# A two-layer trunk on one core: the filling of the delta rule in steps of three matmuls, the gate part inside its own group, and the first value projection in banks 0 and 1

## The chip, the core and the metric

The kernel runs on one core of a Trainium2 chip. The metric is the device time of one execution in microseconds (us). Before the change the median of 3 runs is 1593.56 us (1591.74 to 1597.66). Engines are named as in the profile: PE is TensorE, DVE is VectorE, ACT is ScalarE, POOL is GpSimd and SP is SyncE, whose queue issues most DMAs.

## What is computed

256 tokens of width 1024 pass through two layers and a final RMSNorm, all in float32.

```
layer 0:  x = x + sliding-window attention(rmsnorm(x));  x = x + dense SwiGLU(rmsnorm(x))
layer 1:  x = x + gated DeltaNet(rmsnorm(x));            x = x + top-2-of-8 expert SwiGLU(rmsnorm(x))
```

The change lies in layer 1. Of the DeltaNet, these lines of the reference matter:

```
proj = h @ w_in                                   # 1024 -> q, k (1024 each), v (2048), z (2048), beta, a
qkv = silu(causal_depthwise_conv(qkv, conv_w))    # width 4
a_low = strict lower part of (k_beta @ k.T) * decay, in chunks of 64 tokens, per head
t_inv = inverse of (eye + a_low)
u = t_inv @ (v * beta);  w = t_inv @ (k_beta * exp(gc))
v_new = u - w @ state;  o = q_dec @ state + attn @ v_new;  state = state * decay + k_tail.T @ v_new
o = rmsnorm(o) * norm_g * silu(z);  x = x + o @ w_o
```

## The kernel before

**Dense matmuls.** A weight matrix comes in panels of 128x2048 numbers (1 MB). ACT rounds a panel into `whi` (L627), DVE makes the rest `wlo` (L930), each with three slots, so a panel can be split only when the panel three before it has been used by PE. A product is the sum of three 128x512 matmuls (`triple`, L1421 to L1423). I call such a triple a step. Four steps, one token block against one panel, are a block, and two blocks (b = 0, 1) use up a panel. `AHEAD` says how many panels ACT and DVE split at each place of a group.

**The DeltaNet.** 16 value heads are worked on in four groups of four heads (g = 0 to 3). A group needs 12 blocks of projection, `project(g, i)`: i = 0 to 3 are q and k, 4 to 7 the values v, 8 to 11 the gate z. All are accumulated in PSUM banks 6 and 7 (b = 0, 1). They are copied out with the factor of the RMSNorm: q and k into `group_part(g)` and v into `prj_v` by ACT (L757), z over q and k in `group_part(g)` by DVE (L1088, `z_scaled`), whose SiLU ACT takes in place (L783). A group's output is four blocks of `w_o`, also in banks 6 and 7, which DVE adds to X (L1101).

**The chain of a group.** PE, DVE, ACT and POOL work on one chain: transposes of the projections (L1720), four taps of the convolution (ACT L781, DVE L1110), SiLU, transposes back (L1734, L1746), sums for the decay (L1741), norms, `kk` (L1761), the transposed `qdec` that POOL makes (L1766), the matrix A and its first inverse (DVE, L1773). Then come six levels (lv = 1 to 6), each of which doubles the size of the inverted blocks. A level, for two halves q of the heads:

```
P:   4 matmuls q=0 (L1789)   T: 4 transposes q=0 (L1797)   P: q=1   T: q=1
     DVE copies P into Pc (L1190), ACT copies T into Tc (L826)
     ... filling(6 + lv) ...
dTT: 8 matmuls, both halves (L1807); DVE subtracts them from TT (L1201, four instructions)
     ACT copies even columns of the new TT into Ec (L822), which the next T reads
```

After the levels come the new values, wT, the state and the outputs o, again with copies by ACT (vnew, L833) and DVE in between.

**The filling.** PE does not stand still at these places, because `filling(place)` issues blocks there that do not belong to the chain: the next group's projection and the group before's output. `FILLED[g][place]` is the number of blocks issued by that place, so the finest unit is a block. Groups 0 to 3 hold 12, 16, 16 and 4 blocks. The first group's 12 blocks of projection stand ahead of all this, with 15 products of zeros (`keep_clock`, L1495) between block 3 and block 4, which waits until ACT has emptied banks 6 and 7. Two more such runs (5 and 14 products) stand at the start of group 3.

**The experts.** 8 experts follow, three weight matrices each of 1024x3584. Their panels stream through 14 ring slots straight from HBM; PE uses them as float32 with 32-column tiles (L1884, L1901). SP issues the first ones when the last group's outputs are done (L426, L430). Once per expert, `row_numbers` (L1910) multiplies a 128x144 table, of which one expert's 6 columns are needed. At the end the last expert's rows are added to X by 24 small matmuls (L1988) and DVE (L1403), then squares, rsqrt on POOL (L505), the scaling of both token blocks on DVE (L1412) and two stores.

## Time and profile before

| | |
|---|---|
| median of 3 runs | 1593.56 us (1591.74 to 1597.66) |
| the profiled execution's own time | 1595.22 us |
| its span, first to last instruction | 1593.4 us |
| mean granted clock of TensorE | 0.988 of full speed |
| busy PE / DVE / ACT / POOL | 1529.0 (96%) / 561.5 (35%) / 381.2 (24%) / 185.2 us (12%) |
| chain that ended last | PE 86%, DVE 7%, ACT 3%, POOL 1% |
| moved from and to HBM | 440.87 MB read, 7.34 MB written, 283 GB/s on average |

Three things help in reading it. First, a float32 matmul appears as two instructions (x8 is four matmuls), a triple of fp32r matmuls as three. Second, the duration of a matmul runs until its end leaves the array, while the next one starts long before: what a matmul costs is the distance between two starts. So a stretch can be called busy and still hold time in which PE issues nothing. Third, the profile puts the DeltaNet between 317.7 and 667 us and the experts between 703 and 1578 us; the groups 0 to 3 begin at 346.0, 423.7, 513.2 and 602.4 us.

### The profile page before, as it was taken

How to read it: one execution, taken by the hardware profiler on the slowest of the kernel's cores; microseconds unless marked ns; L12 is line 12 of the kernel's file. 1: busy time of each engine (PE TensorE's matmuls, PEld its weight loads, DVE VectorE, ACT ScalarE, POOL GpSimd, SP SyncE). 2: the span in 40 equal slices, each digit the busy share in tenths (PEclk: the TensorE clock that was granted, in tenths of full speed). 3: DMA queues.
4: the chain of work that ended last, by engine and by line, in shares of the span. 5: the costliest groups of instructions: out<-in, count | busy, mean ns of one | idle time of the engine just before them, and what ended most of it. 6: DMA issues, size and time to landing. Idle time of an engine off the chain costs nothing.

```text
span 1593.4 us, 34961 instructions
## 1 busy us (share of the span) xinstructions
PE 1529.0 (96%) x15647; PEld 912.5 (57%) x15647; DVE 561.5 (35%) x807; ACT 381.2 (24%) x605; POOL 185.2 (12%) x182
## 2 busy tenths in 40 slices
PE   8799999998999998899999999999999999999997
PEld 6677888776877776763443533534444435335344
DVE  4655454557675848342121211212021212111113
ACT  5544444454554535310000000000000000000000
POOL 0100000106152524200000000000000000000100
PEclk9899999999999999999999999999999999999999
DMA  9227555543233200199999999999999999999993
GB/s 349 88 66 258 188 192 184 193 141 114 71 106 101 86 1 1 45 412 415 405 412 407 411 409 408 410 410 408 409 412 398 413 409 405 412 386 412 414 407 137
DMA packets 145354, 450.38 MB, mean 283 GB/s; under 512 B 10624, under 2 KB 41888, under 8 KB 130880
## 3 DMA queue, kind: packets, MB, share of 16 engines
q1 hardware_dynamic: 141680, 437.10, 71.1%
q0 software_dynamic: 3536, 11.14, 1.8%
q8 instruction: 123, 2.02, 0.5%
q14 instruction: 15, 0.12, 0.0%
HBM read 440.87 MB, written 7.34 MB: 281 GB/s over the span
## 4 chain that ended last, share of the span: by engine, by line
PE 86%; DVE 7%; ACT 3%; POOL 1%; SPq 1%; issue 1%; DMA 1%; DVEq 0%; POOLq 0%; ACTq 0%
PE banks L1884 36%; PE banks L1901 18%; PE banks L1421 8%; PE banks L1423 7%; PE banks L1422 7%; PE banks L1797 2%; PE banks L1807 1%; DVE cvall L1110 1%; DVE wlo L930 1%; ACT whi L627 1%; DMA par<-in_attn_sinks_dram 1%; DVE TT L1201 1%; PE banks L1789 1%; PE banks L1841 1%; POOL qdec L539 1%
## 5 line engine op out<-in xcount | busy, mean ns | idle before, releaser
L1884 PE MATMUL banks<-ring,xg 128*32 128x512 f32 (+1 forms) x6144 | 583.2, 539 | 0.0
L1884 PEld LDWEIGHTS banks<-ring,xg 128*32 128x32 f32 x6144 | 199.1, 110 | 367.9 <-issue 331.3
L1246 DVE TENSOR_TENSOR ehid<-banks,esil 64x768 f32<-64x768 f32 (+1 forms) x64 | 89.5, 1398 | 715.1 <-ACT esil L859 714.6
L1901 PE MATMUL banks<-ring,ehT 128*32 128x256 f32 x5376 | 296.1, 379 | 0.0
L1901 PEld LDWEIGHTS banks<-ring,ehT 128*32 128x32 f32 x5376 | 173.6, 110 | 122.3 <-issue 9.7
L859 ACT ACTIVATE esil<-banks 64x1536 f32<-64x1536 f32 (+1 forms) x32 | 41.0, 1282 | 777.9 <-PE banks L1884 777.9
L930 DVE TENSOR_TENSOR wlo<-raw,whi 128x2048 fp32r<-128x2048 f32 x74 | 178.6, 2415 | 77.4 <-ACT whi L627 77.0
L1421 PE MATMUL banks<-whi,xhi 128*128 128x512 f32 x448 | 180.9, 404 | 8.5 <-issue 2.3
L1423 PE MATMUL banks<-whi,xlo 128*128 128x512 f32 x448 | 175.9, 393 | 0.0
L1422 PE MATMUL banks<-wlo,xhi 128*128 128x512 f32 x448 | 175.7, 392 | 0.0
L627 ACT CAST whi<-raw 128x2048 fp32r<-128x2048 f32 x74 | 141.2, 1908 | 49.0 <-PE banks L1423 43.6
L1421 PEld LDWEIGHTS banks<-whi,xhi 128*128 128x128 f32 x448 | 84.6, 189 | 30.0 <-issue 4.9
L1423 PEld LDWEIGHTS banks<-whi,xlo 128*128 128x128 f32 x448 | 84.7, 189 | 18.3
L1422 PEld LDWEIGHTS banks<-wlo,xhi 128*128 128x128 f32 x448 | 84.8, 189 | 16.1
L502 POOL TENSOR_SCALAR par<-par 128x4 f32<-128x4 f32 (+2 forms) x17 | 3.3, 195 | 475.9 <-ACT squares L641 245.7
L585 POOL TENSOR_TENSOR rowcol<-par 128x1 f32<-128x1 f32 x8 | 1.6, 198 | 372.6 <-ACT yrow L876 372.6
L593 POOL TENSOR_TENSOR rowcol<-par 128x1 f32<-128x1 f32 x7 | 1.3, 191 | 365.6 <-DVE next_rows L1304 365.6
L1201 DVE TENSOR_TENSOR TT<-TT,banks 128x128 f32<-128x128 f32 x96 | 22.3, 284 | 59.6 <-PE banks L1807 59.1
L1110 DVE SCALAR_TENSOR_TENSOR cvall<-banks,par,cvall 128x255 f32<-128x255 f32 (+2 forms) x96 | 39.5, 474 | 0.6
L1421 PE MATMUL banks<-whi,hhi 128*128 128x512 f32 x88 | 34.9, 397 | 1.4 <-DVE hlo L1044 1.4
L1422 PE MATMUL banks<-wlo,hhi 128*128 128x512 f32 x88 | 34.7, 395 | 0.0
L1423 PE MATMUL banks<-whi,hlo 128*128 128x512 f32 x88 | 34.7, 394 | 0.0
(304 smaller groups left out, 1296.5 us busy)
## 6 DMA issues: line engine op xcount, KB each, us to landing
ring<-in_moe_w_gate_dram SPq DMA_DIRECT2D x112, 1024.0 KB, 14.8
ring<-in_moe_w_up_dram SPq DMA_DIRECT2D x112, 1024.0 KB, 15.5
ring<-in_moe_w_down_dram SPq DMA_DIRECT2D x112, 1024.0 KB, 14.2
raw<-in_dn_w_in_dram SPq DMA_DIRECT2D x16, 1024.0 KB, 5.1
raw<-in_ffn_w_gate_dram SPq DMA_DIRECT2D x22, 512.0 KB, 4.0
raw<-in_ffn_w_up_dram SPq DMA_DIRECT2D x22, 512.0 KB, 5.0
raw<-in_ffn_w_down_dram SPq DMA_DIRECT2D x11, 1024.0 KB, 4.9
raw<-in_dn_w_in_dram SPq DMA_DIRECT2D x16, 512.0 KB, 4.9
```

Source lines behind the costliest of these rows:

```text
L627: act.copy(slot(whi, n, SPLIT), slot(raw, n, RAW)).then_inc(hi_ready, 1)
L859: act.activation(esil[64:P, :, 0:n_], src[0:64, :, 0:n_], ACT.Silu).then_inc(sem("esil_ready"), 1)
L930: dve.tensor_tensor(slot(wlo, n, SPLIT), slot(raw, n, RAW), slot(whi, n, SPLIT).bitcast(F32), ALU.subtract).then_inc(lo_ready, 1)
L1110: i = dve.scalar_tensor_tensor(out=cvall[:, t, s_:], in0=conv_src(t)[:, 0:SEQ - s_], scalar=tap(g, t, w), in1=cvall[:, t, s_:], op0=ALU.mu ...
L1201: dve.tensor_tensor(t_, t_, d_, ALU.subtract).then_inc(sem("TT_ready"), 1)
L1246: i = dve.tensor_tensor(ehid[64 * s:64 * s + 64, 0:TILES * n_ // 2].rearrange("p (t k j) -> p t k j", t=TILES, k=k_), by_row(src, s), by_r ...
L1421: pe.matmul(ps, lhs_hi, wh, start=start, stop=False)
L1422: pe.matmul(ps, lhs_hi, wl, start=False, stop=False)
L1423: return pe.matmul(ps, lhs_lo, wh, start=False, stop=stop)
L1797: i = pe.matmul(bank[q][64 * b:64 * b + 64, h % 2 * P:(h % 2 + 1) * P], (Ec if lv < LEVELS - 1 else TT)[:, 4 * b + h, 0:64], ident, start= ...
L1884: last = pe.matmul(bank[first_bank + t][TILE * q:TILE * (q + 1), 0:n_].rearrange("p (s c) -> p s c", s=2), xg[:, t, kt, :], w[q // 2][:, k ...
L1901: i = pe.matmul(token_tile(3, t, q, 256), eT[:, h_:h_ + TILE], w[:, at_:at_ + 256], start=first and m == 0 and k == 0 and t % 2 == 0, stop ...
```

## The change

1. **Filling in steps.** `FILLED` now counts steps (triples). Inside a level there are two places, one between T and dTT as before and a new one after dTT. There are two late places, after wT and before the second block's new values. The matmuls of a level stand in the order P, P, T, T instead of P, T, P, T.
2. **Gate part in its own group.** Blocks 8 to 11 of `project(g, i)` are the first four blocks of group g's filling, rather than part of what stands ahead of it. Groups 0 to 3 now hold 48, 64, 64 and 32 steps (12, 16, 16 and 8 blocks); ahead of group 0 stand 8 blocks instead of 12. The order of the panels follows.
3. **Copies.** z goes through one ACT instruction per block straight from PSUM, scale and SiLU together (`gate_silu`), after the second convolution SiLU; DVE's `z_scaled` is gone. DVE copies v (`projected_v`), once per group, before its work on the second block's outputs. ACT copies q and k one block at a time, in levels 2 and 3. DVE adds the second half of an output one block at a time.
4. **First group.** Its v blocks go to banks 0 and 1, so block 4 waits for no copy. The 15 products of zeros are gone, and so are the 5 and 14 in group 3.
5. **ahead(9)**, the late split of a panel on ACT and DVE, stands behind the copy of the second block's new values instead of ahead of it.
6. **Experts.** `row_numbers` multiplies only the 6 columns that are needed.
7. **End.** DVE makes a part of `ylast`. The 24 matmuls go through the four row tiles in turn instead of tile by tile; DVE adds 512 columns at a time (4 instead of 8). ACT scales block 0 of the result, DVE block 1, and DVE multiplies block 0 by the gain while POOL makes the rsqrt.

The diff's core:

```diff
-        FILLED = ((2, 3, 4, 5, 6, 7, 7, 8, 9, 10, 11, 12, 12, 12), (2, 3, 4, 5, 6, 8, 9, 10, 11, 12, 13, 14, 15, 16),
-                  (2, 3, 4, 5, 6, 8, 9, 10, 11, 12, 13, 14, 15, 16), (0, 0, 1, 2, 3, 4, 4, 4, 4, 4, 4, 4, 4, 4))
-        AHEAD = ((4, 5, 6, 6, 7, 7, 8, 8, 9, 9), (4, 5, 6, 7, 8, 8, 9, 9, 10, 11), (4, 5, 6, 7, 8, 8, 9, 9, 10, 11),
-                 (3, 3, 4, 4, 4, 4, 4, 4, 4, 4))
+        STEPS = 4
+        FULL_GROUP = ((8, 12, 16, 20, 24, 29, 32), ((34, 36), (38, 40), (42, 44), (46, 48), (50, 53), (56, 58)), (61, 64))
+        FILLED = (((8, 12, 16, 20, 22, 25, 26), ((27, 28), (30, 32), (33, 35), (36, 38), (39, 41), (43, 44)), (46, 48)),
+                  FULL_GROUP, FULL_GROUP,
+                  ((6, 10, 16, 20, 24, 25, 26), ((27, 27), (28, 28), (29, 29), (30, 30), (31, 31), (32, 32)), (32, 32)))
+        QK_BLOCK0, OUT_BLOCK0 = (1, 2, 3, 5), (4, 6, 7)
+        QK_PART_AT, OUTPUTS_AT = (2, 3), ((0, 0), (4, 5), (4, 5), (3, 6))
+        AHEAD = ((4, 5, 6, 6, 6, 7, 7, 7, 8, 9), (4, 5, 6, 7, 7, 8, 8, 9, 10, 11), (4, 5, 6, 7, 7, 8, 8, 9, 10, 11),
+                 (4, 5, 6, 6, 6, 6, 6, 6, 6, 6))
...
-            def projected(g, part):
-                act.wait_ge(panel_used, PROJ[g, 2 * part + 1] + 1)
...
+            def projected_qk(g, b):
+                act.wait_ge(*((panel_used, PROJ[g, 1] + 1) if b else (sem("block0_psum"), QK_BLOCK0[g])))
+                act.activation(group_part(g)[:, b, :], bank[6 + b], ACT.Copy, scale=rs[:, b:b + 1])\
+                    .then_inc(sem("prj_qk_ready"), 1)
+
+            def first_projected_v():
+                act.wait_ge(panel_used, PROJ[0, 3] + 1)
+                for b in range(TB):
+                    i = act.activation(prj_v[:, b, :], bank[b], ACT.Copy, scale=rs[:, b:b + 1])
+                i.then_inc(sem("prj_v_ready"), 1)
+
+            def gate_silu(g):
+                act.wait_ge(panel_used, PROJ[g, 5] + 1)
+                for b in range(TB):
+                    i = act.activation(group_part(g)[:, b, :], bank[6 + b], ACT.Silu, scale=rs[:, b:b + 1])
+                i.then_inc(sem("z_ready"), 1)
...
-                    if more and lv == 1:
-                        projected(g + 1, 1)
+                    for b in range(TB):
+                        if more and lv == QK_PART_AT[b]:
+                            projected_qk(g + 1, b)
...
+            dve.wait_ge(panel_used, final * EP + (P_MOE + EP))
+            dve.tensor_copy(ylast[:, 512:768], bank[4][:, 0:256]).then_inc(sem("ylast_ready"), 1)
...
+                    i_ = triple(bank[b if first_v else 6 + b], *xT(kt, b), nn, slice(k * 512, (k + 1) * 512), kt == 0, kt == KT - 1)
+                if STEPS - 1 in steps:
+                    if b == 1:
+                        i_.then_inc(panel_used, 1)
+                    elif m == 1:
+                        i_.then_inc(sem("block0_psum"), 1)
...
-            for i in range(12):
-                if i == 4:
-                    keep_clock(15, bank[0])
...
+                def fill_to(count):
+                    while done[0] < count:
+                        k, first = divmod(done[0], STEPS)
+                        end = min(STEPS, first + count - done[0])
+                        steps = range(first, end)
+                        if k < 4:
+                            project(g, 8 + k, steps)
+                        elif g == 0:
+                            project(1, k - 4, steps)
+                        elif g == GROUPS - 1:
+                            output_between(g - 1, k - 4, steps)
+                        elif k in (4, 5, 10, 11):
+                            output_between(g - 1, k - 4 if k < 6 else k - 8, steps)
+                        else:
+                            project(g + 1, k - 6 if k < 10 else k - 8, steps)
+                        done[0] += end - first
...
-                if g == GROUPS - 1:
-                    pe.wait_ge(sem("z_scaled"), GROUPS)
-                    keep_clock(5, bank[6])
                 if g:
                     outputs_T(g - 1)
                 filling(1)
-                if g == GROUPS - 1:
-                    keep_clock(14, bank[6])
...
+                    for q in range(2):
...
-                    filling(6 + lv)
+                    filling_level(lv, 0)
...
+                    filling_level(lv, 1)
...
-                filling(13)
+                filling_late(0)
...
+                        filling_late(1)
...
-                    i = pe.matmul(numbers[:, 0:TURNS * 2 * TILES], sel32[:, b, :], tilerow[:, b, :, :].rearrange("p e t -> p (e t)"),
...
-                for q in range(4):
-                    p_ = slice(TILE * q, TILE * (q + 1))
-                    for t in range(TILES):
...
+                for t in range(TILES):
+                    for q in range(4):
+                        p_ = slice(TILE * q, TILE * (q + 1))
```

In a level of group 1, on PE. Names: `Ac` and `Ec` are even columns of A and TT; L1807 is dTT, L1789 P and L1797 T. Before:

```order
L1422 MATMUL banks<-wlo,xhi 128x512
L1423 MATMUL banks<-whi,xlo 128x512
L1807 MATMUL banks<-Pc,Tc 128x64 x8
L1789 MATMUL banks<-TT,Ac_110 64x64 x4
L1797 MATMUL banks<-tabs,Ec 64x128 x4
L1789 MATMUL banks<-TT,Ac_110 64x64 x4
L1797 MATMUL banks<-tabs,Ec 64x128 x4
L1421 MATMUL banks<-whi,xhi 128x512
```

With the change (L1849 is dTT, L1830 P, L1839 T, L1452 to L1454 a step):

```order
L1849 MATMUL banks<-Pc,Tc 128x64 x8
L1452 MATMUL banks<-whi,xhi 128x512
L1453 MATMUL banks<-wlo,xhi 128x512
L1454 MATMUL banks<-whi,xlo 128x512
L1452 MATMUL banks<-whi,xhi 128x512
L1453 MATMUL banks<-wlo,xhi 128x512
L1454 MATMUL banks<-whi,xlo 128x512
L1830 MATMUL banks<-TT,Ac_110 64x64 x8
L1839 MATMUL banks<-tabs,Ec 64x128 x8
L1452 MATMUL banks<-whi,xhi 128x512
```

Two steps moved from between T and dTT to between dTT and the next P; the other two stayed.

The start of group 3 on PE, before:

```order
L1720 MATMUL banks<-tabs,oall_92 128x128 x8
L1720 MATMUL banks<-tabs,prj_v 128x128 x8
L1495 MATMUL banks<-spare 128x512 x5
L1685 MATMUL banks<-tabs,oall_91 128x128 x8
L1495 MATMUL banks<-spare 128x512 x14
L1734 MATMUL banks<-tabs,cvall 128x128 x8
```

With the change:

```order
L1766 MATMUL banks<-tabs,oall_92 128x128 x8
L1766 MATMUL banks<-tabs,prj_v 128x128 x8
L1452 MATMUL banks<-whi,xhi 128x512
L1453 MATMUL banks<-wlo,xhi 128x512
L1454 MATMUL banks<-whi,xlo 128x512
```

Where the zeros stood there are six steps of the gate part, and four more behind the transposes of the outputs.

ACT in group 1, levels 1 to 3 (L822 and L842 are Ec, L826 and L846 Tc, L627 and L635 the split of a panel). Before:

```order
L822 COPY Ec<-TT 128x128 x4
L826 COPY Tc<-banks 128x256 x2
L757 ACTIVATE prj_v<-banks,par 128x512 x2
L627 CAST whi<-raw 128x2048
L822 COPY Ec<-TT 128x128 x4
L826 COPY Tc<-banks 128x256 x2
```

With the change:

```order
L842 COPY Ec<-TT 128x128 x4
L846 COPY Tc<-banks 128x256 x2
L635 CAST whi<-raw 128x2048
L842 COPY Ec<-TT 128x128 x4
L846 COPY Tc<-banks 128x256 x2
L764 ACTIVATE oall_91<-banks,par 128x512
L842 COPY Ec<-TT 128x128 x4
L846 COPY Tc<-banks 128x256 x2
L764 ACTIVATE oall_91<-banks,par 128x512
```

No more than one of the two kinds of work now stands between a level's copies and the next level's.

## Rows read from the trace of the kernel before

**Rows 1.** Windows: stretch, its length, busy us (instructions) per engine; clock, DMA share, GB/s

```profile
317.70:346.00 28.30, 26.56 (x117) 21.21 (x117) 12.70 (x11) 14.21 (x15) 2.04 (x2) 1.00 0.44 152
346.00:381.10 35.10, 29.84 (x153) 23.70 (x151) 32.90 (x46) 22.37 (x29) 16.72 (x12) 1.00 0.42 137
381.10:414.40 33.30, 31.60 (x349) 25.18 (x349) 15.81 (x39) 15.17 (x37) 9.54 (x8) 1.00 0.30 96
423.70:461.00 37.30, 36.00 (x187) 28.97 (x185) 34.77 (x51) 23.41 (x41) 19.31 (x15) 1.00 0.18 57
461.00:500.20 39.20, 35.82 (x361) 28.37 (x360) 17.52 (x43) 16.57 (x34) 8.47 (x7) 0.96 0.33 108
513.20:602.40 89.20, 82.99 (x630) 67.77 (x628) 59.26 (x98) 45.08 (x88) 32.35 (x24) 0.98 0.15 48
602.40:635.70 33.30, 27.46 (x145) 21.25 (x143) 27.51 (x50) 18.04 (x34) 13.91 (x14) 1.00 0.00 1
635.70:657.20 21.50, 18.57 (x289) 15.84 (x289) 12.79 (x39) 8.99 (x32) 8.04 (x7) 0.92 0.01 2
703.30:1578.00 874.70, 874.70 (x11559) 377.66 (x11558) 140.21 (x164) 49.19 (x51) 48.18 (x62) 1.00 1.01 402
```

**Rows 2.** Waits of PE from 346 to 667 us: total us, times, longest

```profile
PE banks L1841 <- ACT vnew L833: 4.4, 4, 1.5
PE banks L1797 <- ACT Ec L822: 3.7, 2, 1.8
```

**Rows 3.** Timeline, level 4 of group 1: start, length, engine, line

```profile
482.11 0.45 PE L1789 MATMUL banks<-TT,Ac 128*64 128x64 f32 x8
482.64 0.66 PE L1797 MATMUL banks<-tabs,Ec 128*64 128x128 f32 x8
483.13 0.40 PE L1789 MATMUL banks<-TT,Ac 128*64 128x64 f32 x8
483.36 0.61 PE L1797 MATMUL banks<-tabs,Ec 128*64 128x128 f32 x8
483.90 0.50 PE L1421 MATMUL banks<-whi,xhi 128*128 128x512 f32 x1
484.23 0.39 PE L1422 MATMUL banks<-wlo,xhi 128*128 128x512 f32 x1
...
486.86 1.11 PE L1807 MATMUL banks<-Pc,Tc 64*128 64x64 f32 x16
487.57 0.93 DVE L1201 TENSOR_TENSOR TT<-TT,banks 128x128 f32<-128x128 f32 x4 [3.47 <-PE banks L1807]
488.11 0.45 PE L1789 MATMUL banks<-TT,Ac 128*64 128x64 f32 x8
```

**Rows 4.** Timeline, the zeros in the first group's projection, and DVE's first taps

```profile
317.74 3.56 PE L1495 MATMUL banks<-spare 128*128 128x512 f32 x15
...
348.42 5.01 DVE L1110 SCALAR_TENSOR_TENSOR cvall<-banks,par,cvall 128x255 f32<-128x255 f32 x12
```

**Rows 5.** Groups of the page, the split of a panel on DVE and on ACT

```profile
L930 DVE TENSOR_TENSOR wlo<-raw,whi 128x2048 fp32r<-128x2048 f32 x74 | 178.6, 2415 | 77.4 <-ACT whi L627 77.0
...
L627 ACT CAST whi<-raw 128x2048 fp32r<-128x2048 f32 x74 | 141.2, 1908 | 49.0 <-PE banks L1423 43.6
```

**Rows 6.** Chain that ended last, around the first row_numbers: start, length

```profile
703.30 10.44 PE banks L1884 x96
714.43 31.04 PE banks L1884 x288
```

**Rows 7.** Timeline, the end: last expert's rows added, both blocks scaled

```profile
1579.32 5.35 PE L1988 MATMUL banks<-ylast,selTr 32*128 32x256 f32 x48 [0.98 <-ACT ylast L876]
...
1587.85 2.48 DVE L1412 SCALAR_TENSOR_TENSOR H<-X,par,gain 128x1024 f32<-128x1024 f32 x2 [1.20 <-POOL par L505]
```

**Rows 8.** Windows of 2 us, before the clock falls in group 1 and after

```profile
466.00:468.00 2.00, 1.00 (x18) 0.72 (x16) 0.88 (x4) 2.00 (x3) 0.00 (x0) 1.00 0.44 171
...
470.00:472.00 2.00, 2.00 (x17) 1.57 (x15) 1.32 (x3) 1.09 (x3) 0.99 (x1) 0.50 0.06 12
```

More of the change, by code:

```diff
@@ L296, in out_panel @@
             panels.append((dn_w_o[g * 512:g * 512 + 512, h * 512:h * 512 + 512].rearrange("(k p) n -> p k n", p=P),))
-        for m in range(6):
+        for m in range(4):
             project_panel(0, m)
@@ L302, in trunk @@
             LIST.append(len(panels))
-            for m in range(6):
+            for m in (4, 5):
+                project_panel(g, m)
+            for half in range(2):
+                if g:
+                    out_panel(g - 1, half)
                 if g + 1 < GROUPS:
-                    project_panel(g + 1, m)
-                if g and m in (1, 3):
-                    out_panel(g - 1, m // 2)
+                    project_panel(g + 1, 2 * half)
+                    project_panel(g + 1, 2 * half + 1)
         for h in range(2):
@@ L1687, in outputs_T @@
                     i.then_inc(sem("on_psum"), 1)
-            for i in range(12):
-                if i == 4:
-                    keep_clock(15, bank[0])
+            for i in range(8):
                 project(0, i)
```

169 lines of the change are left out of this document (84 added, 85 removed).

## The prediction

> **What bounds the kernel now.** I looked first at the chain that ended last: 86% of it is PE. So I took windows by stage [rows 1]. From 703.3 to 1578 us, in the experts, PE is busy for all of 874.7 us: nothing upstream is hidden there, and what the DeltaNet gives back shows in full at the end, since SP starts the experts' weights when the last group's outputs are done. In the DeltaNet's windows PE is busy for 82 to 97%, which looks like little to gain. The waits [rows 2] name only a few us: 4.4 us in front of L1841 (ACT's copy of vnew) and 3.7 us in front of L1797 (Ec). The timeline of one level [rows 3] shows why this understates it. From 482.11 to 488.11 a level takes 6.00 us. Its filling, 12 matmuls, runs from 483.90 to 486.86. Then dTT's 16 instructions start at 486.86, DVE begins to subtract 0.71 us later, and P can start only at 488.11, 1.25 us after dTT. P's 8 instructions are issued in 0.23 us (483.13 to 483.36), so dTT's 16 take some 0.46 us. The other 0.8 us PE issues nothing, though it counts as busy. A second hole is between P and T of q = 0: 0.53 us where the issue takes 0.23. This pattern stands in all 24 levels. That is what the finer filling is aimed at; PE's own work is the floor.
>
> **Prices.** A 128x512 matmul costs 0.23 us: 15 zeros in 3.56 us, of which the last one's end is 0.4 [rows 4]. A step is then 0.69 us and a block 2.76 us. The block in the level took 2.96 us, and its first matmul 0.33 instead of 0.23 [rows 3]: going into and out of a filling costs about 0.2 us. A bare level's own issue is P 2 x 0.23, T 2 x 0.49 (483.36 to 483.90, less some of the switch) and dTT 0.46, together 1.90 us; with two fillings of 0.2 and 0.05 for the rest, 2.35 us plus 0.69 per step.
>
> **A rule that speaks against two fillings per level.** T, the steps, dTT and P use the array in different tilings (128x64, 128x128, 64x128, 128x64), and the change makes four changes of tiling per level out of three. By [rows 3] the pair of changes costs 0.2 us. The Trainium skill (TensorEngine Tiling, Key Properties) says that a change of the tiling mode drains TensorE. If each change cost the whole tail of a matmul (0.39 of duration less 0.23 of distance), a filling would cost 0.32 us, 24 levels 2.9 us more, and the sum would end at 1557.8 instead of 1554.9 us. The row is a measurement of just these changes, so I keep 0.2.
>
> **The sum, stage by stage.**
>
> *First group's projection, 317.7 to 346.0.* 28.3 us for 8 blocks and the zeros [rows 1]. Four blocks stay (11.0 us, no wait for a copy) and the sums for the gates (0.3): 11.3, so **-17.0 us**. Of this 11.0 is only moved: the four gate blocks are in group 0's filling now, and each later group's likewise, which leaves one group's four blocks extra in group 3. Real gains here are the 15 zeros (3.5) and the waits.
>
> *Group 0, 346.0 to 423.7.* Its start is bound by the chain on DVE, not by PE: DVE is busy for 32.9 of 35.1 us [rows 1]. From the first tap at 348.42 [rows 4] to the first level at 381.1 are 32.7 us. One split of a panel stood between the two halves of the taps (2.3 us and 0.8 idle before it); it is ahead of them now, so 29.8. But the taps begin later after the group's start than the 2.4 us of before. The last v matmul is at 328.7, then ACT copies (1.3), splits a panel (1.9), DVE splits it (2.3) [rows 5] and has 0.3 of small work: taps at 334.5, levels at 364.3, with 0.7 for POOL's qdec 365.0. That is 36.0 us from the start of the group at 329.0 instead of 35.1: +1.0 rounded. The levels: 6 x 2.35 + 18 x 0.69 + 0.5 (levels too short for a DVE split) = 27.0 against 33.3: -6.3. After them four steps more: 2.8 + 0.2 = +3.0. Together **-2.3**.
>
> *Groups 1 and 2.* The start of group 1 (37.3 us) holds 36 steps now and 32 with the change: -2.8 if PE sets it. But what was behind kk (A, T, T0 on DVE and PE) has a chain of its own, so I take -2.3; the ends are 0 and -2.8. Levels: 6 x 2.35 + 26 x 0.69 = 32.0 against 39.2: **-7.2**. Of that some 1.6 is the clock (0.96 in this window [rows 1]): it fell to half after two us in which PE was busy 1.00 of 2.00 us, waiting for an Ec that stood on ACT behind a copy of v and a split [rows 2, 8]. With the change no such pair stands there. After the levels: vnew's copy of the second block no longer waits behind ahead(9) (longest wait 1.5, -0.9), two steps more (+1.4) and the second late filling's entry (+0.1): +0.6. Group 1 **-8.9**. Group 2 has the same length as group 1 (89.2 us [rows 1]), the same tables and waits: **-8.9**.
>
> *Group 3.* 16 steps more and 19 zeros fewer. Its start (33.3 us, PE busy 27.5, including zeros of 4.4) has 26 steps where 16 were: +6.9 - 4.4 of PE work in 5.8 us of idle time, and the same chain on DVE (27.5 of 33.3 busy), which still begins behind the second block's outputs. -0.4; the ends are -1.5 and +2.5. The levels held no filling after the second; now one step each, and with so little the wait behind dTT stays: 0.69 + 0.2 - 0.1 (the new order of P and T) = 0.8 per level, +4.8; of the clock (0.92, so 1.7 us) and the first level's wait I take 1.2 back: +3.6 on 21.5. **+3.2**. The adds of the earlier outputs that DVE moved to levels 3 and 6 are 0.6 us each beside this.
>
> *Experts.* Between two expert products row_numbers takes 714.43 - 713.74 = 0.69 us [rows 6]. With 6 columns each of its four instructions still costs about the 0.11 us of a small one (48 in 5.35 us in [rows 7]), 0.44 together; 8 times 0.25 is **-2.0**. Ends: 0 and -5.5. The weights' stream would have to keep up; the DMA share is 1.01 in that window, PE waits for no weights, and 0.25 us in 109 is nothing.
>
> *End.* DVE takes ylast's smaller part, -0.35. PE's 24 matmuls take 5.35 us in order of tiles [rows 7]; with four row tiles in turn between 2.7 (twice as dense, the density of the experts' column tiles) and 5.35. Then four adds of 512 columns, 0.62 each by the 2.48 us for twice 1024: the last ends some 4.2 us after PE's start, before 5.9. -1.7. The first block's scaling goes to ACT, so the last store is issued 1.2 us earlier, but both stores share the DMA: -0.7. **-2.8**; ends 0 and -3.8.
>
> Sum: -17.0 - 2.3 - 8.9 - 8.9 + 3.2 - 2.0 - 2.8 = **-38.7 us**. Against the profiled execution's own 1595.22 us that is 1556.5 (its span of 1593.4 becomes 1554.7). The median of the runs, 1593.56, is 1.7 below that execution, so I predict **1554.9 us**.
>
> **Rivals.**
>
> *The in-order queues pay part of it back (0.20).* ACT and DVE take a panel's split of 1.9 and 2.3 us in one piece, and a level is to shrink from 6.0 to about 5.1. In a level with both a split and an add on DVE, Pc comes at about 0.7 + 0.9 + 2.3 + 0.6 + 0.5 = 5.0 us after dTT. If Pc or Ec is late by 0.6 us in the 18 levels of groups 0 to 2 (+10) and group 0's start is 5 us longer because POOL's qdec finds less filling in front of it (22 steps instead of 24), the time is 1570. For it: DVE is busy for 33 of 35 us in group 0's start. Against: within the levels it is busy for 17.5 of 39.2 us.
>
> *Everything uncovered (0.05).* If the chain also shortens by what it waited for PE, group 3's levels cost nothing for their steps (-4.8), the starts of groups 1 and 2 give all (-1.0) and group 0's start is 3 us shorter: 1546.
>
> *DVE's chain sets the groups (0.08).* Then the filling moves but the groups do not shorten, and only the zeros ahead of group 0 (3.6), the experts' 2.0 and the end's 2.8 are gained: 1585, at the edge of no change. Against it: in group 1 PE's idle time before its levels is 1.3 of 37.3 us, and levels take 6.00 us with a filling block that alone is 2.96.
>
> *The clock (0.03), slower.* 34 products of zeros that kept PE active go, at the entrance of the layer and in group 3. Where PE was sparsely used the granted clock fell to half, 1.2 GHz: after the 1.00 of 2.00 us of [rows 8]. If group 0's start and group 3 ran at that level, every step there would cost 0.69 us more. With 26 + 32 steps that is 40 us, and another 18 for the chain's own matmuls: 1613. It decides once the doubling costs more than the 38.7 gained plus 8. Against: real steps take the zeros' place, and in group 3's start, idle for 5.8 us, the clock stayed at 1.00. The Trainium skill (TensorE: Matmul & The Clock Gate, What's actually happening) says that the throttled state is the default and activity releases it; by that rule the zeros' removal alone would be the danger, and the filling in their place the cure.
>
> My forecast takes the remaining 0.64.
>
> **Numbers.** The range goes from 1546 to 1573: below, the uncovered case; above, the in-order rival with the bounds of group 3 and the end added. Faster by over 0.5% (8 us, about what a measurement of this kernel can tell from no change): the forecast, the first two rivals and a part of the third, 0.92; within 0.5%: 0.05; slower: 0.03.
>
> **What would show it.** Right: levels of groups 1 and 2 of about 5.1 us each, with P starting straight behind the second filling; group 0 starting at about 329 and first level at about 365; no clock below 1.00 in group 1's levels; groups of about 80 us; the experts unchanged but for 0.4 us between L1884 and L1901 with the numbers. Wrong: levels over 5.5 us with waits for Pc or Ec, group 0's first level later than 370, or a clock under 0.9 over a whole group. If the levels are right and the time isn't, look at PE's wait for POOL's qdec and for A.

## The result, and the profile after

The changed kernel takes 1573.04 us (median of 4 runs, 1571.4 to 1576.36), the kernel before 1595.20 on the same chip (4 runs, 1591.74 to 1597.66). The ratio is 0.9861, 95% interval 0.984 to 0.9882: 22 us, 1.4% faster. The sign was forecast, the size not: -22 us instead of -38.7, and 1573.04 lies just beyond the range's upper end of 1573.

The windows by stage of the changed kernel (stretch, length, busy us and instructions of PE, PEld, DVE, ACT, POOL, then clock, DMA share, GB/s) answer to [rows 1]:

```profile
317.70:329.05 11.35, 11.35 (x54) 9.38 (x52) 6.93 (x7) 9.07 (x11) 2.04 (x2) 1.00 0.57 201
329.05:365.08 36.03, 28.95 (x148) 22.27 (x146) 32.91 (x47) 22.59 (x31) 16.78 (x12) 1.00 0.40 130
365.08:395.80 30.72, 30.09 (x343) 23.10 (x343) 13.77 (x39) 13.61 (x36) 8.64 (x8) 1.00 0.21 70
395.80:407.55 11.75, 11.07 (x85) 10.37 (x85) 6.04 (x7) 5.19 (x13) 4.65 (x4) 1.00 0.28 91
407.55:443.19 35.64, 34.02 (x175) 26.56 (x173) 34.12 (x50) 21.67 (x38) 18.59 (x14) 1.00 0.27 89
443.19:478.73 35.54, 35.54 (x367) 27.64 (x367) 19.27 (x43) 17.36 (x38) 9.69 (x9) 1.00 0.39 119
478.73:491.85 13.12, 12.45 (x92) 11.50 (x91) 5.36 (x7) 5.19 (x13) 3.95 (x3) 1.00 0.26 81
...
576.09:612.47 36.38, 30.77 (x156) 23.85 (x155) 34.04 (x50) 21.63 (x38) 18.51 (x14) 0.95 0.00 1
612.47:637.37 24.90, 23.55 (x306) 18.42 (x306) 12.17 (x39) 8.92 (x32) 8.01 (x7) 0.93 0.01 2
637.37:646.60 9.23, 8.55 (x73) 8.22 (x73) 2.62 (x4) 3.39 (x12) 1.20 (x2) 1.00 0.00 0
```

Each group has three rows: its start, its levels, what follows them. In group 1's levels PE is busy for 35.54 of 35.54 us and the profile names no wait of PE there, and still they take 35.5 us, not the 32.0 of the forecast. In group 3's start PE is busy for 30.77 of 36.38, with a clock below 1.00. Against before:

| stretch | forecast | measured | of it |
|---|---|---|---|
| first group's projection | -17.0 | -16.9 | 28.3 to 11.35 |
| group 0 | -2.3 | +0.8 | start 36.0 as forecast, levels 30.7 for 27.0 |
| group 1 | -8.9 | -5.2 | start 35.6 for 35.0, levels 35.5 for 32.0 |
| group 2 | -8.9 | -5.0 | as group 1 |
| group 3 | +3.2 | +6.5 | start 36.4 for 32.9, levels 24.9 for 25.1 |
| from its outputs to the experts | 0 | 0.0 | |
| experts | -2.0 | -1.2 | 0.54 us per row_numbers, 0.44 forecast |
| end | -2.8 | -1.0 | |
| sum | -38.7 | -22.0 | spans 1593.4 and 1571.4 |

One level of group 1 with four steps, the changed kernel's timeline (start, length, engine, line, operation), for [rows 3]. The weight loads (PEld) are shown with it:

```profile
454.62 0.55 PEld L1830 LDWEIGHTS banks<-TT,Ac 128*64 128x64 f32 x16 [0.36 <-issue]
454.62 0.69 PE L1830 MATMUL banks<-TT,Ac 128*64 128x64 f32 x16
...
455.14 1.05 PE L1839 MATMUL banks<-tabs,Ec 128*64 128x128 f32 x16
...
456.12 0.50 PE L1452 MATMUL banks<-whi,onhi 128*128 128x512 f32 x1
...
457.70 0.97 PEld L1849 LDWEIGHTS banks<-Pc,Tc 64*128 64x128 f32 x16 [0.37 <-issue]
457.71 1.11 PE L1849 MATMUL banks<-Pc,Tc 64*128 64x64 f32 x16
458.42 0.93 DVE L1229 TENSOR_TENSOR TT<-TT,banks 128x128 f32<-128x128 f32 x4 [2.77 <-PE banks L1849]
...
458.75 0.50 PE L1452 MATMUL banks<-whi,onhi 128*128 128x512 f32 x1
...
460.34 0.45 PE L1830 MATMUL banks<-TT,Ac 128*64 128x64 f32 x8
```

From P to P it is 0.52 for P, 0.98 for T, 1.59 for a filling of two steps, 1.04 for dTT (457.71 to 458.75) and 1.59 again: 5.72 us. P and dTT both have 16 matmuls with 64 moving columns; P's weight loads of 64 columns take 0.55 us together, dTT's of 128 columns 0.97. The kernel before had the same row, which I hadn't read:

```profile
486.86 0.97 PEld L1807 LDWEIGHTS banks<-Pc,Tc 64*128 64x128 f32 x16 [0.35 <-issue]
488.10 0.31 PEld L1789 LDWEIGHTS banks<-TT,Ac 128*64 128x64 f32 x8 [0.28 <-DVE TT L1201]
```

So of the 1.25 us between dTT and P [rows 3] 1.04 were dTT itself, and the hole that a second filling can hide was 0.2 us, as much as going into and out of that filling costs.

### The profile page after: what moved, and what is told of

Read it like the earlier page. It is cut to its first block, busy times and chain, and to the rows that moved or that the text cites. A ratio compares the mean times of both kernels' runs of the same rounds, so it can differ in the third digit from the quotient of the medians.

```text
span 1571.4 us, 34876 instructions
## 1 busy us (share of the span) xinstructions
PE 1516.2 (96%) x15613; PEld 897.7 (57%) x15613; DVE 560.7 (36%) x802; ACT 378.9 (24%) x603; POOL 189.1 (12%) x182
## 4 chain that ended last, share of the span: by engine, by line
PE 86%; DVE 8%; issue 2%; ACT 1%; SPq 1%; DMA 1%; POOL 1%; POOLq 0%; DVEq 0%; ACTq 0%
PE banks L1929 37%; PE banks L1946 19%; PE banks L1452 8%; PE banks L1454 7%; PE banks L1453 7%; PE banks L1849 1%; PE banks L1839 1%; DVE cvall L1139 1%; DVE wlo L955 1%; PE banks L1830 1%; DMA par<-in_attn_sinks_dram 1%; DVE T L1199 1%; SPq L409 1%; PE banks L1886 1%; PE banks L1858 0%
## 5 line engine op out<-in xcount | busy, mean ns | idle before, releaser
L1452 PE MATMUL banks<-whi,xhi 128*128 128x512 f32 x448 | 183.0, 409 | 4.6 <-issue 2.3
L1454 PE MATMUL banks<-whi,xlo 128*128 128x512 f32 x448 | 176.1, 393 | 0.0
L635 ACT CAST whi<-raw 128x2048 fp32r<-128x2048 f32 x74 | 141.1, 1906 | 47.1 <-PE banks L1454 41.8
L1452 PEld LDWEIGHTS banks<-whi,xhi 128*128 128x128 f32 x448 | 84.7, 189 | 24.7 <-issue 5.4
L1454 PEld LDWEIGHTS banks<-whi,xlo 128*128 128x128 f32 x448 | 84.6, 189 | 18.5
L1452 PE MATMUL banks<-whi,hhi 128*128 128x512 f32 x88 | 34.9, 397 | 1.4 <-DVE hlo L1069 1.4
L1454 PE MATMUL banks<-whi,hlo 128*128 128x512 f32 x88 | 34.7, 394 | 0.0
```

Source lines behind the costliest of these rows:

```text
L635: act.copy(slot(whi, n, SPLIT), slot(raw, n, RAW)).then_inc(hi_ready, 1)
L1452: pe.matmul(ps, lhs_hi, wh, start=start, stop=False)
L1454: return pe.matmul(ps, lhs_lo, wh, start=False, stop=stop)
```

## Experiments

14 kernels, on several chips. A kernel is compared with the kernel before on the same chip, by the ratio; the changed kernel's experts take 873.6 us on one chip and 881 to 885 on others, so traces are compared stage by stage ahead of them. Where a table or a sentence says "groups", it is the time from group 0's first transpose to the transposes of group 3's outputs: 324.7 us before, 321.9 in the changed kernel.

### One filling or two, and the order of P and T

`one_filling` removes the last line of a level:

```diff
                         i.then_inc(sem("dTT_psum"), 1)
-                    filling_level(lv, 1)
```

> The changed kernel with the filling behind dTT left out in all 24 levels: its steps go to the next level's filling behind T (the last two of a group to the place after the levels), the order P, P, T, T stays. The same steps in all, 18 fillings fewer. Theory A (PE's own work: dTT's 16 instructions cost 1.04 us and the hole behind them is only 0.2, as much as going into and out of a filling costs): a level with four steps stays at 5.7 us from P to P, the time within 3 us of the changed kernel's 1573. Theory B (my prediction's price: dTT 0.46, hole 0.8): levels of 6.3 us, 18 times 0.6 = 11 us longer, 1584. Theory C (the second filling is what keeps Ec and the clock from getting in the way): waits for Ec behind ACT's splits come back in some levels and the granted clock falls in groups 1 and 2, 3 to 6 us longer, with the undisturbed levels at 5.7.

`alternate_order` removes the second loop over q:

```diff
                         i.then_inc(sem("P_psum"), 1)
-                    for q in range(2):
                         if lv < LEVELS - 1:
                             pe.wait_ge(sem("Ec_ready"), ...)
```

> The changed kernel with P and T in the order of before, P T P T instead of P P T T, with both fillings kept. Theory A (the 0.3 us between P and T of before was the wait for Ec, which the filling behind dTT now covers as well): a level of four steps stays at 5.7 us, 1573, within 1 us. Theory B (the order itself costs, by changing between P and T three times instead of once): 0.3 per level, 24 levels, 7 us longer, 1580.

`one_filling_alternate` has both edits.

> Both undone together, so that a level is built as before (P T P T, one filling), all else as changed. Theory A: a level of four steps takes 6.0 us again, 0.3 more than with either alone, 18 times 0.3 = 5.4 us and, in group 3, which had one filling already, 6 times 0.3 = 1.8; with waits for Ec at half clock up to 3 more: 1580 to 1583. Theory B (the fillings were worth 0.6 a level and the order 0.1): 1586 or more. If the effects of the two simply add up from the runs of each alone, their gains are of different causes; by A they don't add, each alone costs nothing.

Starts of P of a four-step level, and the distance to the next:

| | level, us | ratio to before | groups, us |
|---|---|---|---|
| two fillings, P P T T (the change) | 5.71 | 0.9861 (0.9840 to 0.9882) | 321.9 |
| two fillings, P T P T | 5.71 | 0.9848 (0.9831 to 0.9864) | 321.3 |
| one filling, P P T T | 5.93 | 0.9879 (0.9863 to 0.9896) | 326.4 |
| one filling, P T P T | 6.01 | 0.9904 (0.9887 to 0.9920) | 328.6 |

Two levels of `one_filling` in its timeline:

```profile
455.59 1.11 PE L1849 MATMUL banks<-Pc,Tc 64*128 64x64 f32 x16
456.84 0.90 PE L1830 MATMUL banks<-TT,Ac 128*64 128x64 f32 x16
457.56 1.05 PE L1839 MATMUL banks<-tabs,Ec 128*64 128x128 f32 x16
461.52 1.11 PE L1849 MATMUL banks<-Pc,Tc 64*128 64x64 f32 x16
462.77 0.90 PE L1830 MATMUL banks<-TT,Ac 128*64 128x64 f32 x16
```

P follows dTT after 1.25 us as before the change, and P's 16 now stretch from 0.52 to 0.72 us (456.84 to 457.56): its second half waits for TT of the second half of the heads. So one filling costs 0.2 us per level and 4.5 us over the groups, where A expected nothing and B 0.6 per level. The order alone costs nothing while the second filling is there, and 0.1 when it isn't: the 0.3 us between P and T of [rows 3] were a wait for Ec and TT that either edit mostly covers, and the gains of the two don't add up. A holds with a correction of 0.2; B and, in the levels, C don't: the granted clock stayed at 1.00 in both groups' levels. Notice that the level of 9.35 us of before didn't come back in any of the four.

### dTT doubled

```diff
-                        for h in (2 * q, 2 * q + 1):
+                        for h in (2 * q, 2 * q + 1, 2 * q, 2 * q + 1):
                             for b in range(TB):
                                 k_ = slice(64 * b, 64 * b + 64)
```

> The changed kernel with dTT's 16 matmuls of each level issued twice, the same result written again. Theory A (each pair of them costs 0.11 us, since each loads 128 columns of weights): 24 times 0.9 = 21.6 us longer, 1594.6, and the levels of group 1 at 6.6 us. Theory B (0.46 us as for P's 16): 24 times 0.46 = 11 us, 1584, levels at 6.2.

Measured: 1594.49 us, ratio 0.9977 (0.9968 to 0.9987); four-step levels of 6.60 us, 0.90 more. In PE's timeline dTT has 32 matmuls in 2.00 us:

```profile
457.70 2.00 PE L1849 MATMUL banks<-Pc,Tc 64*128 64x64 f32 x32
461.23 0.69 PE L1830 MATMUL banks<-TT,Ac 128*64 128x64 f32 x16
464.31 2.00 PE L1849 MATMUL banks<-Pc,Tc 64*128 64x64 f32 x32
```

A: 0.90 us per level, the price that I had at 0.46. That the time agrees with A's 1594.6 as well is luck: the kernel before took 1598.09 us on this chip, and the groups grew by 20.4 us (342.3 for 321.9), not by 21.6.

### The level of 9.35 us in the kernel before

```diff
-                 ... (4, 5, 6, 7, 8, 8, 9, 9, 10, 11), (4, 5, 6, 7, 8, 8, 9, 9, 10, 11), ...
+                 ... (4, 5, 6, 6, 7, 8, 9, 9, 10, 11), (4, 5, 6, 6, 7, 8, 9, 9, 10, 11), ...
```

(`AHEAD` of groups 1 and 2, in the kernel before.)

> The kernel before with one panel of groups 1 and 2 split a level later (after level 2 instead of level 1), so that ACT has no copy of v and split in a row in front of level 2's Ec. Theory A (of the 7.2 us that each of these groups' levels had over the changed kernel's, 3.3 are one level's wait for Ec and the half clock behind it): the level of 9.35 and 9.15 us becomes 6.0 to 6.3, no clock below 1.00 in groups 1 and 2, 6 us less than before, ratio 0.996. Theory B (the fall of the clock comes from something else, as the zeros or the bursts of the experts' weights): it stays in level 2 or moves to another, the ratio is 0.999 to 1.001.

The 7.2 us in this expectation is the forecast's figure; the levels of group 1 differed by 3.7 (39.2 and 35.5). Measured: ratio 0.9960 (0.9946 to 0.9974), as A said. The levels of group 1 take 5.76, 6.01, 6.01, 5.98, 5.98 and 6.16 us where they took 5.76, 9.35, 6.01, 6.00, 5.99 and 6.15; in the windows of both groups' levels the clock is 1.00:

```profile
461.00:497.00 36.00, 34.32 (x362) 27.23 (x361) 17.75 (x43) 16.63 (x34) 8.22 (x7) 1.00 0.36 118
547.00:583.00 36.00, 34.32 (x362) 27.21 (x362) 17.75 (x43) 16.63 (x34) 8.22 (x7) 1.00 0.09 30
```

Two copies and a split in a row on ACT thus cost 6.5 us in two groups, by a wait of 1.8 us and the half clock behind it. The changed kernel is rid of this since DVE copies v out and ACT's two copies of q and k stand in different levels; that is 3.3 of the 3.7 us that group 1's levels got shorter. No run undoes this part of the change alone; but the level stays away in the four kernels of the table above, whatever their fillings and order.

### P, P, T, T in the kernel before

```diff
                         i.then_inc(sem("P_psum"), 1)
+                    for q in range(2):
                         if lv < LEVELS - 1:
                             pe.wait_ge(sem("Ec_ready"), ...)
```

> The kernel before with P, P, T, T in each level instead of P, T, P, T and nothing else. Theory A, sized by the runs of one filling in either order (5.9 and 6.0 us): 0.1 per level, 2.4 us, the levels with the wait for Ec stay at 9 us: ratio 0.998 to 1.000. Theory B (the whole 0.3 us between P and T of before goes): 7 us, 0.9955.

Measured: ratio 0.9989 (0.9977 to 1.0001), four-step levels of 5.90 us instead of 6.00. The long level of group 1 took 7.54, that of group 2 10.37. A's size; for the time itself a gain isn't told from none.

### Group 3's start

In the changed kernel DVE's timeline shows a panel's split in front of A:

```profile
602.95 2.92 DVE L955 TENSOR_TENSOR wlo<-raw,whi 128x2048 fp32r<-128x2048 f32 x1
605.80 1.27 DVE L1193 TENSOR_TENSOR A<-banks,EB 128x512 f32<-128x512 f32 x2
607.11 2.59 DVE L1199 TENSOR_TENSOR T<-A,tabs 128x512 f32<-128x512 f32 x2
```

In the kernel before DVE had no split between vb and A and waited for kk there:

```profile
629.89 1.29 DVE L1165 TENSOR_TENSOR A<-banks,EB 128x512 f32<-128x512 f32 x2 [4.95 <-PE banks L1761]
631.21 1.75 DVE L1171 TENSOR_TENSOR T<-A,tabs 128x512 f32<-128x512 f32 x2
```

PE's timeline in the changed kernel:

```profile
608.69 0.77 PE L1814 MATMUL banks<-tabs,T 128*128 128x128 f32 x4 [3.12 <-DVE T L1199]
```

PE waits 3.1 us for T. The panel (group 3's first output panel) is not used before the group's end.

```diff
-                 (4, 5, 6, 6, 6, 6, 6, 6, 6, 6))
+                 (4, 4, 5, 6, 6, 6, 6, 6, 6, 6))
```

> The changed kernel with one panel of group 3 split by DVE behind TT instead of in front of A. Theory A (the fifth panel's split, 2.9 us, stands on DVE in front of A while kk is already there at 603.5): A starts 1.9 to 2.3 us earlier, PE's wait of 3.1 us for T shrinks to about 1, and with it goes the fall of the clock behind it, 1.5 us more: group 3 takes 66.5 to 68.5 us instead of 70.5, 1569 to 1571. Theory B (POOL's masks and qdec set this stretch, DVE only waits beside them): A comes earlier but T0 doesn't, no change within 1 us, 1573.

Measured: ratio 0.9831 (0.9815 to 0.9848). DVE's timeline now has A 1.8 us after the add's start, where the changed kernel has 4.1 (601.75 to 605.80):

```profile
600.42 1.28 DVE L1125 TENSOR_TENSOR X<-X,banks 128x512 f32<-128x512 f32 x2
602.21 1.29 DVE L1193 TENSOR_TENSOR A<-banks,EB 128x512 f32<-128x512 f32 x2 [0.51 <-PE banks L1802]
603.53 2.82 DVE L1199 TENSOR_TENSOR T<-A,tabs 128x512 f32<-128x512 f32 x2
```

PE's waits from 560 to 610 us (us in total, times, longest):

```profile
PE banks L1814 <- DVE T L1199: 1.5, 2, 1.1
PE banks L1830 <- DVE TT L1208: 1.4, 1, 1.4
```

The longest wait for T is 1.1 us, a wait of 1.4 for TT is new, and the clock stays at 1.00. Groups: 319.2 us, 2.7 less. Theory A, at the small end of its range. A now starts 27.5 us after the group does, as in the kernel before (27.5; the changed kernel 29.7). Group 3's start takes 34.4 us instead of 36.4, and the 1.1 us that it still is above before's 33.3 are in T: DVE's two operations take 2.82 us here and 2.59 in the changed kernel, 1.75 before. What slows them no run shows.

### Steps moved to the starts

```diff
-        FILLED = (((8, 12, 16, 20, 22, 25, 26), ((27, 28), (30, 32), (33, 35), (36, 38), (39, 41), (43, 44)), ...
+        FILLED = (((8, 12, 16, 20, 24, 26, 28), ((29, 30), (32, 33), (34, 36), (37, 39), (40, 42), (43, 44)), ...
-                  ((6, 10, 16, 20, 24, 25, 26), ((27, 27), (28, 28), (29, 29), (30, 30), (31, 31), (32, 32)), ...
+                  ((6, 10, 16, 20, 24, 26, 29), ((29, 29), (30, 30), (31, 31), (32, 32), (32, 32), (32, 32)), ...
```

with the split moved as well.

> The changed kernel with group 3's split moved as in the run before, two steps of group 0 put in front of kk and two more before its levels, and in group 3 one and four more before the levels (29 instead of 26 of its 32 steps there), so that levels have fewer. Theory A (PE waits in these starts: 3.5 us for qdec, 1.4 for TT, 3.1 for T; a step there is free, and in a level it costs 0.69): group 0 1.5 to 2.5 us shorter, group 3 1 to 2 shorter than with the split alone; 5 to 7 us less than the changed kernel, ratio 0.981 to 0.983 to before. Theory B (what follows only gets later by what is put in): no more than the split's own 2.7 us, ratio 0.984 to 0.9845.

Measured: ratio 0.9834 (0.9814 to 0.9854), groups 316.5 us, 2.7 less than with the split alone: group 0 77.1 us for 78.5, group 3 1.4 less. In the trace A holds, just below and at the small end of its two ranges. In the time it isn't seen: the interval is 0.2% to either side, and between group 3's outputs and the experts this run took 34.15 us where the changed kernel's took 32.5. That stage has the same code in all sixteen kernels. It took 32.5 to 32.6 us in eleven of them, each with a granted clock of 0.95, and 34.1 to 34.2 in five, each with 0.90. So the longer stage goes with a lower clock; what makes the clock fall further in those five is open.

### dTT in quarters

Each pair's load of 128 columns is cut in two, on 64 x 64 tiles:

```diff
-                            for b in range(TB):
+                            for c, b in ((0, 0), (0, 1), (1, 0), (1, 1)):
                                 k_ = slice(64 * b, 64 * b + 64)
-                                i = pe.matmul(bank[2 + 2 * b + q][:, h % 2 * 64:(h % 2 + 1) * 64], Tc[k_, h, :], Pc[k_, h, :],
-                                              start=True, stop=True)
+                                i = pe.matmul(bank[2 + 2 * b + q][64 * c:64 * c + 64, h % 2 * 64:(h % 2 + 1) * 64],
+                                              Tc[k_, h, 64 * c:64 * c + 64], Pc[k_, h, :], start=True, stop=True)
```

> The changed kernel with each of dTT's matmuls cut in two by columns of its weights: 32 of 64 x 64 instead of 16 of 64 rows x 128 columns, the same products and results. Theory A (the load of 128 columns is what a pair waits for, and four quarters load at the pace at which P's pairs of 64 columns do, 0.058 us): dTT takes 0.5 us instead of 1.0, levels of 5.2 us, 24 times 0.5 = 12 us less, 1561. Theory B (quarters of the same rows load one after the other): 16 pairs at 0.058 = 0.93, no change, 1573. Theory C (another tiling mode costs more at each change): above 1575.

Measured: ratio 0.9798 (0.9781 to 0.9814), four-step levels of 5.31 us, groups 312.9 us, 9.0 less. The weight loads of dTT in its timeline:

```profile
448.15 0.56 PEld L1849 LDWEIGHTS banks<-Pc,Tc 64*64 64x64 f32 x32 [0.36 <-issue]
```

Twice the instructions load in 0.56 us instead of 0.97: four quarters start every 0.058 us, as P's pairs do. A in kind; 0.40 per level instead of 0.5. The quarters are tiled by rows too, as dTT's pairs were, so it isn't tiling by rows that costs: what changed is the columns of each load and how many loads run side by side.

### Where the first term comes from

The prediction called the 15 products of zeros [rows 4] a real cost of 3.5 us. `before_no_zeros` is the kernel before without these 15 and the 19 of group 3's start, products that no result uses:

```diff
-                if i == 4:
-                    keep_clock(15, bank[0])
                 project(0, i)
```

> The kernel before without the 15 products of zeros in front of the first group's seventh to twelfth block and without the 5 and 14 in the start of group 3; nothing else changes. Theory A (the first 15 are plain PE work in front of everything, 3.5 us; the other 19, 4.4 us, stand where PE waits for DVE anyway): 3.5 to 4.5 us less than before, ratio 0.9972 to 0.9978, no new fall of the clock. Theory B (they keep the clock up, as their name says): a half clock of 3 us or more appears in the start of group 0 or of group 3, and half or more of the 3.5 is lost: ratio above 0.9985.

Measured: ratio 1.0036 (1.0022 to 1.0051), slower. PE's longest wait in front of group 0 (us in total, times, longest):

```profile
PE banks L1421 <- ACT oall L757: 3.6, 1, 3.6
```

The windows of that wait and of what follows it, columns as in [rows 1]:

```profile
317.70:319.70 2.00, 0.00 (x0) 0.00 (x0) 0.62 (x2) 2.00 (x2) 1.72 (x2) 1.00 0.35 135
319.70:323.10 3.40, 2.64 (x6) 2.17 (x7) 3.34 (x2) 2.50 (x3) 0.32 (x1) 0.57 0.00 0
```

The zeros filled a wait for ACT's copies out of banks 6 and 7, and without them the clock fell to 0.57: group 0 starts at 346.33 us, not earlier than with them (345.95). Group 3's start takes 35.4 us instead of 33.3; its window from 615 to 633 us has a clock of 0.85. In the kernel before, B was right: without the zeros nothing was gained. How much they earned is less clear. In its trace group 0 starts 0.4 us later and is 0.9 us longer, and group 3 is 0.8 us longer: 2.0 together. A further 1.5 us stands in group 2, 1.6 between the groups and the experts, and 2.5 in the last stage (17.9 us for 15.4), where the code is the same and the clock was lower. The last 24 matmuls took 5.35 us in [rows 7] at a clock of 1.00, and here, at 0.66:

```profile
1594.19 7.82 PE L1983 MATMUL banks<-ylast,selTr 32*128 32x256 f32 x48 [0.98 <-ACT ylast L876]
```

`before_split_later`, which has all its zeros, has the same long last stage (18.1 us), so it also comes where no zeros are missing.

Two kernels then take the changed one apart: `v_in_banks_6_7` (`first_v = False`, and ACT reads banks 6 and 7) and `zeros_back` (`keep_clock(15, bank[2])` in front of the fifth block).

> The changed kernel with the first group's value projection in banks 6 and 7 again, and still no zeros in front of it. Theory A (the other banks are the gain: the fifth block no longer waits for ACT to copy the first four out of banks 6 and 7, behind a panel's split): PE waits 3.4 us or more there, the clock falls to half for a window behind it, group 0 starts 4 to 6 us later than 329.05, and the time is longer by that: ratio 0.989 to 0.990 to before. Theory B (the zeros were the cost, as my prediction put it): group 0 starts within 1.5 us of 329, ratio 0.986 to 0.987.

> The changed kernel with the 15 products of zeros back in front of the fifth block (into bank 2), and the value projection in banks 0 and 1 as changed. Theory A (with the other banks nothing is waited for, so that they are plain PE work): group 0 starts 3.5 us later, 332.5, and the time is 3.5 us longer, ratio 0.9883. Theory B (ACT's and DVE's own work in front of group 0 sets its first level, not PE): the first level comes less than 1.5 us later than 365.1, ratio under 0.987.

Measured: ratios 0.9904 (0.9887 to 0.9921) and 0.9888 (0.9872 to 0.9905). Without the other banks PE waits 3.0 us and the clock is at 0.67 behind it; the first level starts at 369.93 us instead of 365.08. With the zeros back it starts at 367.70; their row

```profile
316.70 3.56 PE L1526 MATMUL banks<-spare 128*128 128x512 f32 x15
```

shows that they are plain work there, though they begin a microsecond earlier than the changed kernel gets to this place. A in kind both times, with smaller sizes: group 0 starts 3.7 us later (332.71) instead of 4 to 6, after a wait of 3.0 instead of 3.4, and with the zeros 2.4 later (331.48) instead of 3.5. In both traces the clock also fell in group 0's start (0.91 and 0.95 over it, 1.00 in the changed kernel). The banks take the wait away, and only then are the zeros a cost.

### The last gain

```diff
-            dve.tensor_tensor(H3[:, 0, :], X[:, 0, :], gain3[:, :], ALU.mult).then_inc(sem("gained"), 1)
+            for q in range(8):
+                i = dve.tensor_tensor(H3[:, 0, q * P:(q + 1) * P], X[:, 0, q * P:(q + 1) * P], gain3[:, q * P:(q + 1) * P], ALU.mult)
+            i.then_inc(sem("gained"), 1)
```

> The changed kernel with the multiplication by the last gain (first block, 1024 columns, 1.22 us on DVE) cut into eight of 128 columns. Theory A (POOL's first small operation of the last 1/rms takes 1.08 us instead of 0.18 because it can't get at the memory while DVE's one long operation runs): it takes 0.2 to 0.4 us now, and the last stage becomes 0.4 to 0.8 us shorter (14.4 us from the last expert's product to the end). Theory B (POOL's operation is long for another reason): it stays at 1.1, and the end comes 0.3 to 0.5 us later, by the seven more instructions.

POOL's timeline has its first operation of the last 1/rms. In the changed kernel:

```profile
1563.96 1.08 POOL L510 TENSOR_SCALAR par<-par 128x2 f32<-128x2 f32 x1 [82.37 <-DVE par L1439]
```

In the kernel before:

```profile
1586.75 0.18 POOL L502 TENSOR_SCALAR par<-par 128x2 f32<-128x2 f32 x1 [84.78 <-DVE par L1408]
```

In this one:

```profile
1573.58 0.35 POOL L510 TENSOR_SCALAR par<-par 128x2 f32<-128x2 f32 x1 [83.22 <-DVE par L1439]
```

The last stage takes 13.94 us instead of 14.40. A. The ratio of 2 runs, 0.9857 (0.9833 to 0.9880), can't show it.

### All of it together

> The changed kernel with all that has been tried for it: dTT in quarters, group 3's split later, the steps moved to the starts, the gain in eighths. If the gains add up (dTT 9.0 us within the four groups, split 2.7, steps 3, end 0.5): 15 us less than the changed kernel, 1558, ratio 0.977. If shorter levels only bring out DVE's and ACT's work behind them (a level of 5.3 us with a split on both): 11 us less, ratio 0.979.

Measured: 1570.51 us where before took 1606.83, ratio 0.9778 (0.9761 to 0.9795), groups 308.2 us and the end 13.94. The groups gave 13.7 of the 14.7 us expected, in spite of a new wait of 1.5 us for Pc in group 3; the stage behind them took 34.2 us, 1.7 more than in the changed kernel's trace. The ratio's interval holds both expectations, 0.977 and 0.979; by the groups the gains nearly add up. It is faster than both kernels: 2.2% than before, some 0.8% than the changed one, whose ratio is 0.9861.

## Why the prediction was right in sign and wrong in size

- **"P's 8 instructions are issued in 0.23 us, so dTT's 16 take some 0.46 us. The other 0.8 us PE issues nothing."** This step failed. dTT's 16 take 1.04 us (and `dtt_twice` added 0.90 per level), since they load 128 columns each and P's load 64. A bare level with two fillings is 0.52 + 0.98 + 1.04 + 0.42 = 2.96 us, not 2.35. Six levels of groups 0, 1 and 2 each are 3.6 us longer by it, 10.8 in all: with it alone the forecast would have been 1565.7 us, inside the range. Of the 16.7 us between forecast and measured spans, these are 10.8, group 3's start is 3.5, the end 1.8 and the experts 0.8; the rest nearly cancels. The columns stand in PEld's row; I had read the matmuls' row only. The Trainium skill (TensorE: Matmul & The Clock Gate, LDWEIGHTS (loading the stationary operand)) has the rule: a weight load's time goes by its columns, not by its rows. The traces agree: 0.112 us from pair to pair with 128 columns, 0.058 with 64.
- **The finer filling in the levels** was therefore worth 0.3 us per level of four steps (6.01 to 5.71), not 0.9, and the second filling and the new order largely cover the same waits. Of the 3.7 us that group 1's levels gained, 3.3 came from the level with the wait for Ec. The six finer levels gave 1.8 more, and two more steps took 1.4 of it back. I had seen that pair on ACT and that the change parts it, but priced it at 1.6.
- **"Going into and out of a filling costs about 0.2 us", against the rule that each change of tiling drains TensorE.** Right: a filling of two steps takes 1.59 us, 0.21 more than 1.38. The 0.32 by the rule would have given 1557.8, nearer to the result for a reason that isn't the one.
- **"The same chain on DVE" in group 3's start, -0.4.** Failed by 3.5 us. The chain is the same, but `AHEAD` now puts two splits of 2.9 us behind vb, where DVE was idle for 4.95 us before; the second stands in front of A, which comes 2.2 us later, and T then takes 0.8 us longer. With one entry of the table changed, the start got 2.0 us shorter and the groups 2.7. The rival of the in-order queues named 1570 us, close to the result, but by another way: Pc or Ec late in 18 levels and a start of group 0 that is 5 us longer. PE waits for no Ec now, for Pc once (0.6 us, in group 0), and that start takes 36.0 us as forecast. Only in group 3's start was the rival's kind of delay there, so its number is near by luck.
- **First group's projection, -17.0, and group 0's start, 36.0 us.** Both right (16.9 and 36.0), but the reason was half of it. The sum took 3.5 us for the zeros as a gain of their own and "no wait for a copy" beside it. Taken alone the zeros gain nothing, since they stand in that wait; they are a cost only once the other banks have removed it. The rival of the clock, which had the zeros keep it up, named what happened in the kernel before without them. In the changed one steps stand in their place, and it was wrong: no clock under 1.00 in group 0, and 0.95 and 0.93 in group 3's start and levels, where the levels of before had 0.92.
- **Small terms.** Starts of groups 1 and 2: 0.6 us too low each; what follows the levels of groups 0 to 2: 0.5 too high each. Experts: 0.54 us per row_numbers instead of 0.44, 0.8 in all. The end: the adds finish 5.4 us after the last expert's product instead of 7.2, as forecast, but POOL's small operation gives 0.9 back, taking 1.08 us instead of 0.18 while DVE multiplies, for which the sum had nothing. (The end's 1.0 us is against a trace in which the last 24 matmuls ran at full clock, 15.4 us in all; in two other kernels with the same last stage it took 17.9 and 18.1, and in the changed kernel and its variants never more than 14.4.) And where the last store followed DVE's last scaling by 3.1 us before (1590.3 to 1593.4), it takes 4.2 now (1567.2 to 1571.4): both stores are issued together, so of the 1.2 us of earlier scaling that I counted on 1.1 are lost, not 0.5.
- The rival "everything uncovered" (1546) and "DVE's chain sets the groups" (1585) are out: the first wanted group 3's levels 4.8 us shorter than forecast and group 0's start 3 us shorter, and they took 24.9 and 36.0 us, as forecast; the second wanted groups of the same length, and groups 1 and 2 got 5 us shorter.

## What to carry to other kernels

Before pricing a hole behind a row of small matmuls, read its weight loads: their columns set the pace, and a hole is only what lies beyond them. Where it is weight columns that a small product waits for, smaller tiles that load side by side can cut its time, as they did here from 1.04 to 0.63 us. A filler that stands in a wait costs nothing until the wait is gone, so take out the two together; and when a table lets panels be split earlier, look at what stands behind each split on its queue, and at whether the panel is needed that soon.

## What the runs showed of the hardware

- Loads of weights for 64 x 64 tiles run four at a time at the pace of a pair of 128 x 64: 32 loads in 0.56 us against 16 of 64 x 128 in 0.97.
- A POOL operation on two columns took 1.08 us beside a DVE operation with two inputs in SBUF, 0.18 with DVE idle, 0.35 beside eight short ones; the long one ended at 1565.04, when DVE's operation (from 1563.78, 1.22 us) did. The Trainium skill (SBUF — State Buffer, SBUF: two separate sides) calls the port pair that DVE and GpSimd share an exclusive lock held for a whole instruction, where DVE's has two inputs in SBUF and GpSimd's reads SBUF; these three numbers agree.
- A long PE wait is not always followed by a lower clock, even with the same code. The waits of 3.6 and 3.0 us in front of group 0 were followed by 0.57 and 0.67. The wait of 3.5 us for qdec in group 0's start left the clock at 1.00 in the changed kernel, in every window of 2 us from 352 to 370 us; in `dtt_quarters` and `zeros_back` the same start with the same wait had 0.95.

```profile
358.38 1.09 PE L1807 MATMUL banks<-tabs,qdec 128*128 128x128 f32 x8 [3.49 <-POOL qdec L547]
```

- The fall behind the wait of 3.1 us in group 3's start (0.50 from 610 to 614 us) was gone when that wait shrank to 1.1.
